# mLSTM mixer: a head's four old-state products for the sample go together, behind the next head's numerators

## The reference

```python
num = w_inter[..., None] * jnp.einsum('bhtd,bhde->bhte', q, C) + jnp.einsum('bhts,bhse->bhte', s, v)
nq = w_inter * jnp.einsum('bhtd,bhd->bht', q, n) + jnp.sum(s, axis=-1)
h = num / jnp.maximum(jnp.abs(nq), jnp.exp(-m_t))[..., None]
C_new = g_state[..., None, None] * C + jnp.einsum('bhs,bhsd,bhse->bhde', g_tok, k, v)
n_new = g_state[..., None] * n + jnp.einsum('bhs,bhsd->bhd', g_tok, k)
```

## Time and profile before

| | |
|---|---|
| Median of 3 runs | 1801.85 us (1801.56 to 1803.14) |
| Span of the profiled execution, first to last instruction | 1800.1 us |
| Device time outside a span, by the median | 1.75 us |
| PE / DVE / ACT / POOL busy | 98% / 63% / 49% / 9% |
| Mean granted TensorE clock | 0.996 |
| Two mixers' heads, head 0 to the down projection | about 222 to 303 us and 1449 to 1528.5 us |

### The profile page before, as it was taken

How to read it: one execution, slowest core, us unless ns; L and a number is a source line. 1 busy time by engine, 2 the same in 40 slices (tenths; PEclk the granted TensorE clock), 3 DMA queues, 4 the chain that set the end, 5 groups by cost and what they waited for, 6 DMA issues and landing times.

```text
span 1800.1 us, 33987 instructions
## 1 busy us (share of the span) xinstructions
PE 1763.9 (98%) x13177; PEld 1641.6 (91%) x13177; DVE 1142.0 (63%) x1856; ACT 876.4 (49%) x1470; POOL 160.4 (9%) x111
## 2 busy tenths in 40 slices
PE   7999999999999999999999999999999999999997
PEld 6999855999999979999997799999999955999997
DVE  5886577575556546664576676555887568676543
ACT  4565423455444485554454555544665422455443
POOL 0000132110011002000120020011000034110000
PEclk9999999999999999999999999999999999999998
DMA  5565334555555614555543155555555424555552
GB/s 163 164 168 168 97 117 164 196 163 167 166 167 169 194 54 156 164 163 166 166 120 116 48 162 166 169 169 164 159 163 176 135 93 161 187 161 160 173 166 86
DMA packets 155883, 272.94 MB, mean 152 GB/s; under 512 B 22693, under 2 KB 28274, under 8 KB 155770
## 3 DMA queue, kind: packets, MB, share of 16 engines
q1 hardware_dynamic: 155770, 271.37, 48.4%
HBM read 250.55 MB, written 20.78 MB: 151 GB/s over the span
## 4 chain that ended last, share of the span: by engine, by line
PE 88%; DVE 7%; ACT 3%; DMA 1%; issue 1%; SPq 0%; ACTq 0%; DVEq 0%
PE PS L1787 86%; PE PS L1792 2%; ACT PB L955 1%; DVE C L1339 1%; DVE WLO L1062 1%; DVE QT L1374 0%; DVE NB L1330 0%; DMA XIN<-in_x_sample_dram 0%; DVE TMP L1649 0%; DMA out_p_C_dram<-CPST 0%; DMA RAWT<-in_c_w_ukv_dram 0%; DVE QT L1379 0%; DVE BST L1316 0%; DVE KS L1306 0%; DVE HL L1385 0%
## 5 line engine op out<-in xcount | busy, mean ns | idle before, releaser
L1062 DVE TENSOR_TENSOR WLO<-RAWT,WHI 128x512 fp32r<-128x512 f32 (+1 forms) x904 | 636.2, 721 | 482.0 <-ACT WHI L653 479.9
L653 ACT ACTIVATE WHI<-RAWT 128x512 fp32r<-128x512 f32 (+1 forms) x904 | 555.2, 626 | 646.7 <-PE PS L1787 644.8
L1787 PE MATMUL PS<-XGH,WHI 128*128 128x288 f32 x1776 | 526.8, 297 | 4.7 <-DVE WLO L1062 4.0
L1787 PE MATMUL PS<-HH,WHI 128*128 128x288 f32 (+1 forms) x1792 | 528.7, 295 | 0.4 <-issue 0.4
L1787 PE MATMUL PS<-HH,WLO 128*128 128x288 f32 (+1 forms) x1792 | 528.0, 295 | 0.0
L1787 PE MATMUL PS<-HL,WHI 128*128 128x288 f32 (+1 forms) x1792 | 527.5, 294 | 0.0
L1787 PE MATMUL PS<-XGH,WLO 128*128 128x288 f32 x1776 | 524.1, 295 | 0.0
L1787 PE MATMUL PS<-XGL,WHI 128*128 128x288 f32 x1776 | 523.7, 295 | 0.0
L1787 PEld LDWEIGHTS PS<-XGH,WHI 128*128 128x128 f32 x1776 | 334.2, 188 | 8.2 <-DVE WLO L1062 4.5
L1787 PEld LDWEIGHTS PS<-HH,WHI 128*128 128x128 f32 x1792 | 336.8, 188 | 3.9 <-issue 3.6
L1787 PEld LDWEIGHTS PS<-HH,WLO 128*128 128x128 f32 x1792 | 336.4, 188 | 0.0
(11 more groups left out here) (364 smaller groups left out, 1416.0 us busy)
## 6 DMA issues: line engine op xcount, KB each, us to landing
RAWT<-in_w_ff_dram SPq DMA_DIRECT2D x256, 512.0 KB, 3.7
RAWT<-in_a_w_up_dram SPq DMA_DIRECT2D x64, 512.0 KB, 3.7
RAWT<-in_a_w_down_dram SPq DMA_DIRECT2D x32, 512.0 KB, 3.8
RAWT<-in_b_w_qkv_dram SPq DMA_DIRECT2D x24, 512.0 KB, 3.8
RAWT<-in_a_w_q_dram SPq DMA_DIRECT2D x16, 512.0 KB, 3.7
RAWT<-in_a_w_k_dram SPq DMA_DIRECT2D x16, 512.0 KB, 3.8
RAWT<-in_a_w_v_dram SPq DMA_DIRECT2D x16, 512.0 KB, 3.9
C<-in_state_mlstm_C_dram SPq DMA_DIRECT2D x8, 1024.0 KB, 5.9
```

Source lines behind the costliest of these rows:

```text
L653: act.activation(hi, raw, ACT.Copy).then_inc(weight_hi, 1)
L1062: dve.tensor_tensor(lo, raw, hi, ALU.subtract).then_inc(weight_lo, 1)
L1787: return pe.matmul(out, lhsT, rhs, start=start, stop=stop, **kw)
```

## The change

- `old_state(h)` makes all four products of a head at once, each into a bank of its own: 1, 6, 3, 2 (6, 7, 4, 5 for the last head), in place of two pairs in banks 3 and 2.
- On PE they stand in the next head, right after its numerators and norms and before `sample(h-1)`; the next scores and the next `broadcast` come after them and wait for pieces 0 and 1 of the state on DVE; the second part of the scores and the query-state products come after that, the latter behind all four pieces.
- On DVE `state(h)` is four pieces in a row at the end of a head, ahead of the next head's `spread`; none is left between `spread` and `centre`. Each piece increments `cs_out`.
- `remainders` of head h-1 moves into head h, ahead of `outputs`, where DVE waits for the transposes; that of head 2 stands in the tail after L1415, ahead of the last `outputs`.
- In the last head `new_state(0)` comes after the sample's numerators and waits for two state pieces.
- The last head's four products stand ahead of unit 2 of the down projection; the pair ahead of unit 0 is gone.

```diff
+        def old_bank(h, b):
+            return ((1, 6, 3, 2) if h < AH - 1 else (6, 7, 4, 5))[b]
...
-                        sp.wait_ge(cs_out, 2 * U + 2)
+                        sp.wait_ge(cs_out, 4 * U + 4)
...
-                def state(h, b0):
+                def state(h):
 
                     U = AH * la + h
-                    for b in (b0, b0 + 1):
+                    for b in range(4):
                         dve.wait_ge(cs_done, 4 * U + b + 1)
-                        bank = (3, 2)[b % 2] if h < AH - 1 else (6, 7, 4, 5)[b]
-                        ins = dve.scalar_tensor_tensor(C0[:, h % 2, b, :], C0[:, h % 2, b, :], AECOL[:, 25 + h:26 + h],
-                                                       PS[:, bank, :], ALU.mult, ALU.add)
-                    ins.then_inc(cs_out, 1)
+                        dve.scalar_tensor_tensor(C0[:, h % 2, b, :], C0[:, h % 2, b, :], AECOL[:, 25 + h:26 + h],
+                                                 PS[:, old_bank(h, b), :], ALU.mult, ALU.add).then_inc(cs_out, 1)
...
-                    if h:
-                        state(h - 1, 2)
                     dve.wait_ge(hy_out, U + 1)
...
                         probs(h + 1)
+                        if h:
+                            remainders(h - 1)
                         outputs()
                         keys(h + 1)
-                        remainders()
-                        state(h, 0)
+                        state(h)
...
+                remainders(AH - 2)
                 outputs()
-                remainders()
+                remainders(AH - 1)
...
                     if h:
-                        if not last:
-                            scores(h + 1, (0,))
-                            broadcast(h + 1)
-                        if last:
-                            new_state(0)
-                        pe.wait_ge(cs_out, 2 * U - 1)
-                        old_state(h - 1, 2)
+                        pe.wait_ge(cp_out, 4 * U)
+                        old_state(h - 1)
+                        sample(h - 1)
                     if last:
-                        sample(h - 1)
                         for j in range(AH):
                             mm(PS[32 * j:32 * j + 32, 0, :], PTS[:, j, :], VREP[:, 512 * j:512 * (j + 1)], j == h, j != h,
                                skip_group_check=True)
+                        pe.wait_ge(cs_out, 4 * U - 2)
+                        new_state(0)
                     else:
...
-                            broadcast(1)
+                        else:
+                            pe.wait_ge(cs_out, 4 * U - 3)
+                            scores(h + 1, (0,))
+                            pe.wait_ge(cs_out, 4 * U - 2)
+                        broadcast(h + 1)
                         scores(h + 1, (1,))
                         if h:
-                            sample(h - 1)
-                            pe.wait_ge(cs_out, 2 * U)
+                            pe.wait_ge(cs_out, 4 * U)
...
                         keys(h + 1)
-                        pe.wait_ge(cp_out, 4 * U + 4)
-                        old_state(h, 0)
...
                         if k == 0:
-                            last_state(0)
                             pe.wait_ge(nst_out, la + 1)
                             pe.wait_ge(smh_lo, la + 1)
                         if k == 2:
-                            last_state(2)
+                            last_state()
```

More of the change, by code:

```diff
@@ L1380, in outputs, with remainders @@
                            .then_inc(mo_out, 1)
-                    def remainders():
-                        dve.wait_ge(mh_hi, U + 1)
-                        dve.tensor_tensor(HL[:, H4, 0:TP], QT[:, H4, 0:TP], HH[:, H4, 0:TP].bitcast(F32),
+                    def remainders(x):
+                        f = slice(4 * x, 4 * x + 4)
+                        dve.wait_ge(mh_hi, AH * la + x + 1)
+                        dve.tensor_tensor(HL[:, f, 0:TP], QT[:, f, 0:TP], HH[:, f, 0:TP].bitcast(F32),
                                           ALU.subtract).then_inc(mh_lo, 1)
@@ L1416, in mlstm_mix @@
                    .then_inc(smh_lo, 1)
+                remainders(AH - 2)
                 outputs()
-                remainders()
+                remainders(AH - 1)
                 def last_state():
-                    state(AH - 1, 0)
-                    state(AH - 1, 2)
+                    state(AH - 1)
                 return last_state
@@ L1990, in broadcast, with old_state @@
                     mm(PS[:, 6 if h else 4, 0:T], SEL[:, h, :], R[:, 0:T]).then_inc(bcast_done, 1)
-                def old_state(h, b0):
-                    U = AH * la + h
+                def old_state(h):
                     vh = slice(512 * h, 512 * (h + 1))
-                    for b in (b0, b0 + 1):
+                    for b in range(4):
                         r = slice(32 * b, 32 * b + 32)
-                        bank = (3, 2)[b % 2] if h < AH - 1 else (6, 7, 4, 5)[b]
-                        mm(PS[:, bank, :], KGH[r, h % 2, :], VREP[r, vh]).then_inc(cs_done, 1)
+                        mm(PS[:, old_bank(h, b), :], KGH[r, h % 2, :], VREP[r, vh]).then_inc(cs_done, 1)
                 scores(0)
@@ L2132, in mlstm_mix, with last_state @@
                 xp(PS[0:32, 0, 0:P], NOUT[:].rearrange("p s f -> p (s f)")).then_inc(nst_done, 1)
[L2134 to L2139, removed]
+                def last_state():
+                    pe.wait_ge(cp_out, 4 * U + 4)
+                    pe.wait_ge(hg_out, U + 1)
+                    old_state(AH - 1)
                 pe.wait_ge(cp_out, 4 * U + 3)
@@ L2466, in ready @@
                         if k == AB - 1:
-                            pe.wait_ge(cs_out, 2 * AH * (la + 1))
+                            pe.wait_ge(cs_out, 4 * AH * (la + 1))
                     hh_stage(ST["down", i], ready)
```

## The result

The changed kernel takes 1814.17 us in the median of 4 runs (1811.08 to 1819.19); the kernel before has 1801.7. The ratio is 1.0073, 95% interval 1.0057 to 1.0089: slower by 0.7%. The forecast was 1807.5, and the range ended at 1810.5.

What follows compares the result with a forecast made beforehand. The loop over DVE, ACT and PE was taken to bound the heads. Layer 0 1.85 + 0.85 = 2.7, layer 3 2.0 + 0.85 = 2.85, together +5.6 on 1801.85: 1807.5 us; 8-in-10 range 1804.5 to 1810.5.

Steps and rivals of the forecast that it cites:

- One middle head, +0.70: Heads 1 and 2: DVE's way from `outputs` to `decay` takes 15.72 us against 15.02, so each gets 0.70 longer.
- Head 3 and the tail, +0.45 to +0.6 beyond heads 1 and 2: Last head to down projection: the down projection starts 2.0 us later in layer 3, 1.85 in layer 0.
- The collision with L1749: Head 3: DVE's L1321 or L1322 waits for POOL's L1749, both reading two SBUF tiles; 0 or 0.4 us a layer.
- The down projection, +0.85: Unit 3: `remainders` behind L1415 makes `WLO` 1.13 us later, so PE waits about 0.85 once a layer.
- The removed pair ahead of unit 0: Start of the down projection: removing the pair gives nothing back, since unit 0 also waits for `smh_lo`.
- rival (c): PE's idle time in the heads lowers the clock, or the four products go in series; 1809 to 1813.5 us, chance 0.12.
- The prediction's own sign of being wrong: Heads: under 0.6 us DVE wait before the first piece, products 2 and 3 a microsecond late, or clock below 1.00.
- 929 to 1016 at 1.00 with 79 of 87 us busy: Stretch of the kernel before, with waits all through yet at 2.4 GHz; held against the clock falling in rival (c).

Runs made afterwards that it cites:

- fill_both: Changed kernel plus unused PE products, one ahead of `new_state(1)` in heads 1 and 2, two ahead of the down projection's unit 0; 1808.0 us, ratio 1.0032.
- pair_back: Changed kernel with the last head's first two old-state products ahead of unit 0 of the down projection again; 1810.5 us, ratio 1.0056.
- after_again: The changed kernel itself, unaltered, in six more runs beside another set of the kernel before; 1812.90 us, ratio 1.0068.
- gap_tail: Kernel before with only `remainders` moved into the next head's transpose wait, head 2's into the tail's; 1800.0 us, ratio 0.9993; repeated, 1799.3 us, 0.9992.
- delay: Kernel before with DVE making each `remainders` of heads 0 to 2 twice, products still in pairs; 1809.5 us, ratio 1.0047.
- fill_heads: Changed kernel plus one unused PE product (0.87 us) in heads 1 and 2, in the idle time ahead of `new_state(1)`; 1808.5 us, ratio 1.0034.
- delay_qcp: Kernel before, products in pairs, with ACT making `QCP` three times in heads 1 and 2; 1812.9 us, ratio 1.0065.
- split_pair_tail: Changed kernel with state pieces 2 and 3 behind `spread`, last head's first pair ahead of unit 0, head 2's `remainders` in the tail's wait; 1802.1 us, ratio 1.0002.

## Why the prediction was wrong

- *One middle head, +0.70.* Right in mechanism and nearly in size: first piece late by 1.21 in head 1 (1.33 forecast), four products in 1.07 (1.06), ACT's steps 0.51, head 21.60 instead of 20.83, so +0.77, and PE idle 1.40 (1.25).
- *Head 3 and the tail, +0.45 to +0.6 beyond heads 1 and 2.* Mis-sized. In layer 3 of fill_both and of pair_back, where no fall disturbs it, the way from the start of the heads to unit 0 grew by 1.4 in all, and in layer 0 of after_again by 1.5. That is what heads 1 and 2 give, so head 3 gave nothing. The collision with L1749 (here L1750) did not come: POOL's four multiplications (L1741) take 3.94 where they took 5.0. They also take 3.94 in gap_tail, where only `remainders` was moved away from beside them, and 5.51 in delay, where it stands there twice. So POOL was through before DVE's small steps came:

```profile
287.43 3.94 POOL L1741 TENSOR_SCALAR SX<-SX,COLS 128x256 f32<-128x256 f32 x4
...
291.45 1.27 POOL L1747 TENSOR_TENSOR KT<-HH,HL 128x512 f32<-128x512 f32 x1
...
292.80 1.05 POOL L1750 TENSOR_TENSOR KT<-KT,COLS 128x512 f32<-128x512 f32 x1
...
294.14 0.16 DVE L1324 TENSOR_TENSOR LNS<-MV,LNS 128x2 f32<-128x2 f32 x1
294.33 0.16 DVE L1325 TENSOR_TENSOR LNS<-LNS 128x2 f32<-128x2 f32 x1
```

  (Changed kernel, layer 0; here the falls in heads 1 and 2 had set in too. L1750 ends at 293.85, ahead of L1324.)
- *The down projection, +0.85.* There, at 0.63 of PE's idle time in pair_back and fill_both. In the changed kernel without a fall (layer 0 of after_again) it is 0.33, behind a unit 0 that starts 0.3 later than pair_back's, so the sum is the same. In the profile with a fall in both layers the wait is gone: PE is slower than DVE just then.
- *The removed pair ahead of unit 0.* The schedule argument holds (unit 0 waits for `smh_lo`), the conclusion "nothing" does not: it was PE's only work in a wait of 2.3 to 2.6 us.
- *The step that failed* is the clock, which the sum put at nothing on the strength of the weighing in rival (c). That rival named the mechanism, PE's idle time and even the price of 1.6, but counted one fall or so, and was given, together with products in series, 0.12. There are six places for a fall, heads 1 and 2 and the down projection in each of two layers; five came in the profile of the changed kernel and three in that of after_again, and the loss by the clock rose by 8 to 9.5 us. The prediction's own sign of being wrong, a clock below 1.00 in the heads, was met. The evidence held against the rival, 929 to 1016 at 1.00 with 79 of 87 us busy, was one execution, and another one, of fill_heads, has that stretch at 0.92. It was also a sum over many waits, and did not speak for one of 1.4 us at this place; `delay`, with waits of 0.5 and 0.2, and `delay_qcp`, with one of 1.64, do. The Trainium skill ("TensorE: Matmul & The Clock Gate", Why this matters for your kernels) warns of idle gaps between bursts of matmuls, but only of gaps longer than the waits of 1.4 and 2.3 us behind which the clock fell here; the measurement decides.
- *Sum.* Schedule: 1.4 + 0.65 a layer, about 4; fill_both measures 5.8 (2.9 to 8.5). Clock: the loss rose from between 5.4 and 6.1 to between 14.2 and 15.0, so by 8 to 9.5. Together 12 to 15, and 12.1 to 12.5 were measured. Counted by places instead, with 9 of 16 waits of 1.4 us and 9 of 10 of the longer ones followed by a fall, an execution has some 4 falls, an estimate of 6.5 us at 1.6 each; the schedule of fill_both and these falls make 12.3. Why the loss rose by more than 6.5 is not shown.

## What to carry to other kernels

An operation of PE that frees nothing when it goes may be what keeps PE at full clock; before one takes work off PE or lets one of its waits grow, list where its new idle stretches lie and how long each is. A clock of 1.00 in one profile does not show that a stretch is safe. A price that comes in a part of the executions must be multiplied by the number of places, here three in each of two layers. Gathering products on different rows of the array was cheap on PE (1.07 us for four), but their consumer now waits for them, since they stand behind the next head's numerators: leave pieces beside the other engines' small steps, and a product ahead of the long wait, as `split_pair_tail` does, and the change costs nothing that the runs can tell.

## What the runs showed of the hardware

- Four 32-row products into four banks took 1.07 us from start to the next instruction, as two do.
- After a wait of 1.4 us behind one-column products eight passes took 3.70, 5.24 or 5.40 us; the same instructions and the same wait gave both in one execution. With 0.87 us of it filled by an unused product the clock was 1.00 in all eight such heads of two profiles, and the kernel was 5 us faster.
- A fall came behind 13 of 20 waits of 1.4 to 1.6 us in the heads and 9 of 10 of 2.3 to 3.4 us ahead of unit 0, behind none of 36 in the heads where it was some 0.3 us or less.
- POOL's four one-input multiplications took 3.94 us without DVE's `remainders` (a subtraction of two tiles, 1.13 us) beside them (changed kernel, gap_tail), 5.0 with it (before), and 5.51 with two of them (delay).
